# Two transformer blocks on one core: the recurrent mixer's gate chains are computed one head ahead, and the eight accumulator banks are divided anew

## The reference

```
h = rms_norm(x, attn_norm)
proj = h @ w_in                       # all projections of the layer
o_a = sparse attention, 4 heads of 128, keys chosen by a score (top 128)
o_b = hgrn2_mixer(q, f, i, g)         # 4 heads of 128, below
o_c = latent attention, 4 heads of 128 + 64 rotated
gates = sigmoid(proj[gate columns])   # 3 x 1024 columns
mixed = g_a * (o_a @ w_up_a) + g_b * (o_b @ w_up_b) + g_c * (o_c @ w_up_c)
x = x + mixed @ w_out
h = rms_norm(x, ffn_norm)
x = x + (silu(h @ w_ffn_gate) * (h @ w_ffn_up)) @ w_ffn_down    # width 2816
out = rms_norm(x, final_norm)

def hgrn2_mixer:                      # in chunks of 64 rows, a state per head
    log_f = logaddexp(log lb, log(1-lb) + log_sigmoid(f));  k = (1-lb) * sigmoid(-f)
    b = cumsum(log_f) within the chunk
    attn[t,s] = sum_k q[t] k[s] exp(b[t]-b[s]),  s <= t
    o = (q * exp(b)) @ state + attn @ v
    state = exp(b_last) * state + (k * exp(b_last - b))^T @ v
    out = rms_norm(o) * silu(g)
```

## Time and profile before

| | |
|---|---|
| Median of 3 runs | 2035.2 us (2034.4 to 2037.26) |
| The profiled execution: its time, and its span in the trace | 2032.24 us, 2030.4 us |
| PE busy | 1764.3 us (87% of the span) |
| PE clock granted, mean over the span | 0.933 of full speed |
| DVE, ACT, POOL busy | 847.8, 805.0, 590.5 us (42%, 40%, 29%) |
| Moved by transfers | 149.83 MB |

### The profile page before, as it was taken

One profiled execution on the slowest core, in us unless ns is written; L12 is line 12 of the kernel. 1 busy time (PEld: TensorE's weight loads), 2 busy tenths in 40 slices (PEclk: granted clock), 3 DMA queues, 4 the chain that ended last, 5 costly groups with the idle time before them and its releaser, 6 DMA issues.

```text
span 2030.4 us, 20883 instructions
## 1 busy us (share of the span) xinstructions
PE 1764.3 (87%) x7694; PEld 1325.3 (65%) x7694; DVE 847.8 (42%) x1477; ACT 805.0 (40%) x1512; POOL 590.5 (29%) x291
## 2 busy tenths in 40 slices
PE   4899998889989988889979968867769879999997
PEld 3666765667757656676636657656557658888886
DVE  4363345453433453544983536242326312212401
ACT  2234447322344563433324545453443324434411
POOL 4332211144122211422201222131236424444540
PEclk8898999999989988899989989888879989999999
DMA  5312221023132201231212222221245323333221
GB/s 172 88 42 63 63 59 57 22 64 93 32 82 54 83 32 43 88 82 33 60 36 58 73 73 63 60 66 48 66 132 185 103 62 100 98 94 101 86 94 42
DMA packets 204115, 149.83 MB, mean 74 GB/s; under 512 B 14956, under 2 KB 183536, under 8 KB 204016
## 3 DMA queue, kind: packets, MB, share of 16 engines
q1 hardware_dynamic: 199488, 133.57, 23.3%
q0 software_dynamic: 4528, 14.95, 2.4%
HBM read 138.00 MB, written 10.49 MB: 73 GB/s over the span
## 4 chain that ended last, share of the span: by engine, by line
PE 69%; DVE 13%; ACT 8%; issue 4%; DMA 3%; SPq 1%; POOL 0%; ACTq 0%; DVEq 0%
PE proj L1436 39%; PE proj L1432 12%; PE attn_out L1602 3%; PE score L1559 3%; PE score L1622 2%; PE turned_probs L1588 2%; PE proj L1622 1%; ACT weights_rounded L1900 1%; PE attn_out L1622 1%; DMA weights_raw<-in_w_in 1%; DVE small L2157 1%; DMA gates<-constants 1%; SPq L1316 1%; DVE rel_bias L2070 1%; PE score L1563 1%
## 5 line engine op out<-in xcount | busy, mean ns | idle before, releaser
L1378 POOL TENSOR_TENSOR weights_rounded<-weights_raw,weights_rounded 128x1024 fp32r<-128x1024 f32 (+1 forms) x237 | 562.8, 2392 | 1140.3 <-ACT weights_rounded L1900 1140.2
L1436 PE MATMUL proj<-hT_high,weights_rounded 128*128 128x512 f32 x2336 | 785.7, 410 | 47.4 <-DVE weights L2325 16.6
L1436 PEld LDWEIGHTS proj<-hT_high,weights_rounded 128*128 128x128 f32 x2336 | 456.9, 196 | 163.3 <-issue 20.4
L1436 PE MATMUL proj<-hT_low,weights_rounded 128*128 128x512 f32 x1168 | 468.9, 401 | 0.0
L1900 ACT ACTIVATE weights_rounded<-weights_raw 128x1024 fp32r<-128x1024 f32 (+1 forms) x237 | 233.9, 1009 | 161.1 <-DMA weights_raw<-in_w_ffn_down 57.8
L1436 PEld LDWEIGHTS proj<-hT_low,weights_rounded 128*128 128x128 f32 x1168 | 229.2, 196 | 50.4 <-issue 4.7
L1432 PE MATMUL proj<-weights_rounded,hT_high 128*128 128x512 f32 (+1 forms) x640 | 212.3, 409 | 43.8 <-DVE hT_low L1981 21.0
L1432 PEld LDWEIGHTS proj<-weights_rounded,hT_high 128*128 128x128 f32 x640 | 127.9, 203 | 77.3 <-issue 23.4
L1588 PE MATMUL turned_probs<-constants,probs 128*128 128x128 f32 x320 | 62.1, 296 | 43.4 <-ACT probs_T L1792 43.0
L1640 ACT ACTIVATE tg<-proj 128x512 f32<-128x512 f32 x42 | 25.1, 598 | 177.0 <-PE proj L1436 177.0
L1559 PE MATMUL score<-qk 64*128 64x256 f32 (+3 forms) x256 | 81.0, 495 | 11.0 <-DVE qk L1975 8.2
(11 more groups left out here) (371 smaller groups left out, 2463.6 us busy)
## 6 DMA issues: line engine op xcount, KB each, us to landing
weights_raw<-in_w_in SPq DMA_DIRECT2D x113, 512.0 KB, 4.1
weights_raw<-in_w_out SPq DMA_DIRECT2D x24, 512.0 KB, 3.8
weights_raw<-in_w_ffn_gate SPq DMA_DIRECT2D x22, 512.0 KB, 3.8
weights_raw<-in_w_ffn_up SPq DMA_DIRECT2D x22, 512.0 KB, 3.8
weights_raw<-in_w_ffn_down SPq DMA_DIRECT2D x22, 512.0 KB, 3.6
gates<-constants POOLq DMA_DIRECT2D x24, 256.0 KB, 2.4
weights_raw<-gates SPq DMA_DIRECT2D x24, 256.0 KB, 3.9
weights_raw<-in_w_in SPq DMA_DIRECT2D x20, 256.0 KB, 3.1
```

Of the source, the lines that this page charges most:

```text
L1378: nc.gpsimd.tensor_tensor(piece_view(WR, p, "raw"), piece_view(WF, p, "raw"), piece_view(WR, p, "high"), ALU.subtract).then_inc(w_low, 1)
L1436: mm = nc.tensor.matmul(ps[:, :], w_[:, c0:c0 + P], x_[:, k, :], start=first, stop=last)
```

## The change

Four things change together.

1. Until the last stage the projections have three banks and the scores two, instead of two and three.
2. The mixer stage is written by hand (`paced`): each job has a fixed number of ticks behind it. The hf and hq groups and the gate chain of head h + 1 stand among the levels of head h, with second copies of k, b and q (`by_head`). The put of a level stands ahead of the next level's work, and a `sigmoid` or projection group stands between most dependent steps, where state, out and meansq stood closer together. The mixer stage holds 22 gates, and two are left for the last stage.
3. In the last stage the groups go round all eight banks.
4. The first feed-forward chunk is done in two parts: the 384 columns of the first three row tiles before the last tile is turned (`early`), and 128 columns after it.

The steps of the first block and of the score stage keep their order.

```diff
-PROJ_BANKS = 2
-SCORE_BANKS = 3
+PROJ_BANKS = 3
+SCORE_BANKS = 2
+BANKS = 8
...
+    def paced(jobs, new_items):
+        add_items(new_items)
+        for fn, ticks in jobs:
+            fn()
+            for _ in range(ticks):
+                if state["n"] < len(items) + DRAIN:
+                    tick()
...
+    def hgrn_turn(h):
         put_back()
-        hold["put"] = g
+        group("hg_turn", head=h)
+        if h < 3:
+            steps.append(("hg_diff", (h + 1, 0)))
...
+    for h in range(4):
+        last = h == 3
...
+        level(-1, 1)
+        jobs.append((lambda h=h: next_f(h + 1), 0))
+        level(0, 1)
+        jobs.append((lambda h=h: next_q(h + 1), 0))
+        level(1, 0)
+        jobs.append((next_gate, 0))
+        jobs.append((lambda h=h: gate_step(h + 1, ("hg_gate_d", 0)), 0))
+        level(2, 1)
+        jobs.append((lambda h=h: gate_step(h + 1, ("hg_gate_a", 1)), 0))
+        level(3, 0)
+        jobs.append((next_gate, 1))
+        jobs.append((lambda h=h: gate_step(h + 1, ("hg_gate_d", 1)), 0))
+        level(4, 0)
+        jobs.append((lambda h=h: hgrn_gate(h), 1))
+        level(5, 1)
+        jobs.append((lambda: steps.append(("gate2", hold["g"])), 0))
+        jobs.append((next_gate, 0))
+        jobs.append((lambda h=h: hgrn_turn(h), 1))
+        jobs.append((lambda h=h: hgrn_state(h), 1))
+        jobs.append((next_gate, int(last)))
+        jobs.append((lambda h=h: hgrn_out(h), int(last)))
+        if not last:
+            jobs.append((next_gate, 0))
+        jobs.append((lambda h=h: hgrn_meansq(h), int(last)))
+        if not last:
+            jobs.append((next_gate, 0))
+        jobs.append((lambda h=h: hgrn_norm(h), 0))
+    paced(jobs, its)
     flush()
     state["after"] = ("tail", 0)
     steps.append(("tail", 0))
+    steps.append(("split_x", ("ya", 0, 4)))
+    while given[0] < N_GATES:
+        next_gate()
+    new_rings(RINGS_TAIL)
...
+    turned = [group("to_hT", tile=NT - 1, half=half, norm=2 * NT - 1, late=True) for half in range(2)]
+    begun = []
+    for what, name in (("ffgate", "ffg"), ("ffup", "ffu")):
+        sl = slab(name, at=0)
+        used(sl, turned[0])
+        begun.append(group(what, sl, K=KD, ring=0, late=True, cols=P * (NT - 1), **(dict(chunk=0, gate=begun[0]) if begun else {})))
+    steps.extend([("early", g) for g in begun] + [("group", g) for g in turned + begun])
...
+    for g in range(len(groups)):
+        b = g % PROJ_BANKS if tail_group is None or g < tail_group else (g - tail_group) % BANKS
...
-        hF, hA, hK, hQ = (qk[:, 4 + i, :] for i in range(4))
-        hB, hG, hQD, hKE, hATT = (X[:, i, :] for i in range(5))
+        hF, hA = qk[:, 4, :], qk[:, 5, :]
+        hB0, hG, hQD, hKE, hATT = (X[:, i, :] for i in range(5))
+        by_head = [(hB0, qk[:, 6, :], qk[:, 7, :]), (E[:, 0, 1, :], E[:, 1, 1, :], ikT)]
...
+                    elif bank_no[g] >= PROJ_BANKS:
+                        pe.wait_ge(exp_done, len(items))
+                        pe.wait_ge(soft1_done, soft1_at[-1])
+                        pe.wait_ge(turned_out, turned_at[-1])
...
+                    if lv == 0 and h:
+                        dve.wait_ge(group_full, out_group[h - 1] + 1)
```

More of the change, by code:

```diff
@@ L516, in plan @@
     if not only_block1:
-        second(steps, groups, slabs, items, units, state, slab, used, group, turn_rows, wide_tiles, weave, flush, new_rings, rounds)
+        second(steps, groups, slabs, items, units, state, slab, used, group, turn_rows, wide_tiles, weave, paced, flush, new_rings, rounds)
     place_splits(steps, groups, slabs, pieces)
@@ L551, in place_splits @@
         k = max(at.get(seq, -1), start[p["after"]], before)
-        while steps[k + 1][0] not in ("group", "half", "down"):
+        while steps[k + 1][0] not in ("group", "half", "early", "down"):
             k += 1
@@ L561, in place_splits, with second @@
     steps[:] = out
-def second(steps, groups, slabs, items, units, state, slab, used, group, turn_rows, wide_tiles, weave, flush, new_rings, rounds):
+def second(steps, groups, slabs, items, units, state, slab, used, group, turn_rows, wide_tiles, weave, paced, flush, new_rings, rounds):
     l = DEPTH
@@ L655, in hgrn_level @@
             steps.append(("hg_decay", h))
-        g = group("hg_attn", head=h, level=lv)
+        hold["put"] = group("hg_attn", head=h, level=lv)
+    def hgrn_turn(h):
         put_back()
-        hold["put"] = g
+        group("hg_turn", head=h)
+        if h < 3:
+            steps.append(("hg_diff", (h + 1, 0)))
     def hgrn_state(h):
-        group("hg_turn", head=h)
-        put_back()
-        if h < 3:
-            hgrn_q(h + 1)
-        gs = [group("hg_state", head=h, part=i) for i in range(2)]
@@ L666, in hgrn_state @@
-        if h < 3:
-            hgrn_f(h + 1)
-        steps.append(("hg_chain", (h, gs)))
-        hold["states"] = gs
-        if h < 3:
-            steps.append(("hg_gate_a", (h + 1, 0)))
-        hold["g"] = hgrn_gate(h)
-        if h < 3:
-            steps.append(("hg_gate_d", (h + 1, 0)))
+        hold["states"] = [group("hg_state", head=h, part=i) for i in range(2)]
+        steps.append(("hg_chain", (h, hold["states"])))
     def hgrn_out(h):
-        hold["hgout"] = group("hg_out", head=h, states=hold["states"])
@@ L678, in hgrn_out, with hgrn_meansq, hgrn_norm @@
-        if h < 3:
-            steps.append(("hg_gate_a", (h + 1, 1)))
+        group("hg_out", head=h, states=hold["states"])
+    def hgrn_meansq(h):
         group("hg_meansq", head=h)
+    def hgrn_norm(h):
         steps.append(("hg_norm", h))
         steps.append(("gate3", hold["g"]))
-        if h < 3:
-            steps.append(("hg_gate_d", (h + 1, 1)))
-            steps.append(("hg_diff", (h + 1, 0)))
     def hgrn_gate(h):
-        g = group("gate", slab("hgrn", c0=HG + 128 * h), K=KD, chunk=4 + h, layer=l, first=False, unit=None)
@@ L704, in gate_logs, with gate_step, next_f @@
-    def gate_logs(i):
-        if 0 <= i < N_GATES:
-            steps.append(("sig_ln", i))
-    def gate_out(i):
-        if 0 <= i < N_GATES:
-            steps.append(("sig_out", i))
+        put_back()
+        hold["g"] = group("gate", slab("hgrn", c0=HG + 128 * h), K=KD, chunk=4 + h, layer=l, first=False, unit=None)
+    def gate_step(h, *what):
+        if h < 4:
+            steps.extend((name, (h, part)) for name, part in what)
+    def next_f(h):
+        if h < 4:
+            put_back()
+            hgrn_f(h)
@@ L876, in annotate @@
             gr["vals"] = dict(values) if kind.startswith("hg_") else None
+        elif op == "early":
+            groups[arg]["early_hT"] = list(hT_groups)
         elif op == "split_x":
@@ L1250, in two_blocks @@
         ffup_group = [gr["g"] for gr in groups if gr["kind"] == "ffup"]
-        tail_group = next((gr["g"] for gr in groups if gr["kind"] == "up"), None)
         n_swaps = sum(gr["kind"] == "swap" for gr in groups)
@@ L1399, in _ @@
                     pe.wait_ge(prep, N_PREP)
-                elif op in ("group", "half"):
+                elif op in ("group", "half", "early"):
                     gr = groups[arg]
```

131 lines of the change are left out of this document (68 added, 63 removed).

## The result

The changed kernel takes 1960.47 us (median of 4 runs, 1960.21 to 1964.25), against 2036.23 us for the kernel before in runs beside it (4 runs, 2034.4 to 2037.5): ratio 0.9633, 95% interval 0.9616 to 0.965, faster. The forecast was 1948 us, 87 less than before; measured are 76 less. The profiled execution took 1960.21 us with a span of 1958.4 us, 72.0 us under the span of before.

The account below looks back on a forecast made before the run. PE's work plus its waits, densest in the mixer stage, bound the kernel. Mixer stage -82, way in +9, last stage -16 and first block +2 sum to -87 us, giving 1948 us; range 1912 to 1988.

Parts of the forecast that it names:

- Mixer stage: Groups and items ahead of dependent steps cover PE's waits; 9% idle, clock 0.95: 307 us, 82 less (64 to 123).
- the stores' pace: Rival, chance 0.22: in the mixer stage gates' copies wait for stores, costing most of 42 us: 1980 us.
- Way in: From the last `hg_out` to the first `up`: two leftover gates and waits for their weights, 9 us more.
- Last stage: Turned-tile waits gone, early part and split nearly even, some clock regained: 16 us less, 5 to 26.
- with eight banks PE no longer waits for the evacuation of a turned tile: In the last stage, PE's waits of 9.1 + 3.0 us for turned tiles' banks go.
- the 5 that I had counted for the clock: In the last stage, half of the 10 us lost at the lower clock level comes back: 5 us less.
- the late part: In the last stage, 48 matmuls of 128 columns at 0.112 us each take 5.4 us.
- First block: Only its banks change: 8 us for two score banks against 6 for the third projection bank, 2 more.
- The term for two score banks: In the first block, scores wait until the item two before lets go of its bank: 8 us more over two layers.
- The term for the third bank: In the first block, waits for spread rows (5.2) and copied values (3.0) go in part: 6 us less.
- everything is covered: Rival, chance 0.14: mixer stage with 3% idle and clock 0.98 takes 279 us, 28 less: 1920 us.
- the clock staying at 0.89: Rival, chance 0.06: PE's waits shorten but the clock falls as often as before; mixer stage 21 us more: 1974 us.

Follow-up runs that it names:

- experiment 3: The changed kernel with two projection banks and three score banks, in its new order: 1993.37 us, ratio 0.9821 to the kernel before.
- experiment 5: The changed kernel with three places instead of two for the tail gates' values: 1919.87 us, ratio 0.9462 to the kernel before.
- experiment 9: The kernel before, its order and banks kept, with three places for the tail gates' values: 2017.3 us, ratio 0.9935.
- Experiment 8: The changed kernel with its eight banks kept but the first feed-forward product in one part: 1956.74 us, ratio 0.9633 to the kernel before.
- experiment 1: The kernel before with three projection banks and two score banks, nothing else changed: 1988.29 us, ratio 0.9798.
- 4: The changed kernel with three banks in turn to the end and the first feed-forward product in one part: 1956.65 us, ratio 0.9641 to the kernel before.
- experiment 2: The kernel before with two score banks instead of three, the freed bank unused until `down`: 2044.53 us, ratio 1.0074.

## Why the prediction came out near

**Mixer stage: forecast 82 less, measured 60.2.** The mechanism was right: groups and items ahead of the dependent steps took away the waits for the put, the chain, the squares and the gate chain, and order and bank add (46 and 14 us, experiment 3). The step that failed is the one that gave the stores' pace a chance of its own instead of a term: the store's wait is there, and a chain that I held covered, turn, copy, state, hangs behind it. With it gone the stage takes 303.3 us (experiment 5), 101 less than before. That is within the ends of 64 and 123 that I had named. So of 101 us that order, bank and a third place give together, 41 hung on the stores. My price for that rival, 42 us, was right in sum and by luck, as I had 34 of idle time and 8 of the clock, and measured are 21.6 and 19.2. I had also taken its base too high, since idle came to 6% and the clock to 0.98 where I chose 9% and 0.95. Two choices between far ends, both toward the worse, stood in for the wait that I left out of the sum. The old order gained only 13 us by a third place (experiment 9), perhaps as it asked for gates less evenly and PE stood for other chains meanwhile; that last reason is argued, not shown.

**Way in: forecast 9 more, measured 11.3.** I had 8.5 us of PE waiting for the leftover gates' weights and found 12.69. I had listed the copy, the branch's rounding, the logs and exponential, the rounding and POOL. Missing was DVE: its 2.29 us for the branch's low part stand ahead of the gate's minimum, and the logs wait for that:

```profile
1415.70 1.91 ACT L1968 ACTIVATE branches_high<-y 128x2048 fp32r<-128x2048 f32 x1 [1.09 <-DVE y L2109]
...
1417.65 2.29 DVE L2422 TENSOR_TENSOR branches_low<-y,branches_high 128x2048 fp32r<-128x2048 f32 x1 [2.06 <-ACT branches_high L1968]
1419.86 0.69 DVE L2091 SCALAR_TENSOR_TENSOR constants<-constants,gate_logs 128x512 f32<-128x512 f32 x1
1420.63 0.63 ACT L1690 ACTIVATE gate_logs<-constants 128x512 f32<-128x512 f32 x1 [3.02 <-DVE constants L2091]
...
1423.01 1.99 ACT L1952 ACTIVATE weights_rounded<-weights_raw 128x1024 fp32r<-128x1024 f32 x2
...
1426.67 0.76 PE L1488 MATMUL proj<-hT_high,weights_rounded 128*128 128x512 f32 x1 [12.69 <-POOL weights_rounded L1422]
```

ACT's waits of 3.02 us for that chain and of 1.09 for the norm ahead of the branch's rounding are the missing 4.2. The wait ahead of `up` is 2.97 us, forecast near 3. Another of 3.39 us for POOL, 9 us behind the first `up`, I had not foreseen; it lies in the last stage.

**Last stage: forecast 16 less, measured 6.9.** The step that failed is "with eight banks PE no longer waits for the evacuation of a turned tile", taken as worth 9.1 + 3.0 us. These waits are gone, but waits for data stood behind them, and PE waits for those now. Experiment 8 has the eight banks and the product whole, and its list has these:

```profile
PE proj L1478 <- DVE mix_low L2416: 3.6, 3, 3.1
PE proj L1536 <- DVE logits L2308: 3.4, 1, 3.4
```

Its idle time from the first `up` to the first `down` is 18.8 us against 25.7 before, 7 less instead of 12. Its busy time is 5.1 less (364.5 to 359.3), which are the 5 that I had counted for the clock. Nor does it take eight banks: in experiment 1, with three in turn, the stretch from the first `up` to the first feed-forward product is 134.1 us against 146.9 before, and 1.0 us is left of these waits. Eight instead of three bring nothing that can be seen (experiment 8 against 4). The second term that was off is the late part. I had the waits right in kind and nearly in size, 4.81 and 1.67 us for my 4 and 2, but sized the work behind them at the full clock; and they took 10.2 us instead of 5.4. In the profiles the split costs 9.0 us of work against my 2.7 and saves 3.8 of idle time against my 2.0, so a cost of 0.7 became one of 5.2. Of the 6.3 us more work the late part is 4.8. The rule of the Trainium skill that I had set beside this term (TensorE: Matmul & The Clock Gate, Back-to-back issue gap: about 81 ns for 128 columns) was further off than the row: the first products came every 0.11 us at full clock, and 48 in 10.2 us are 213 ns each, most of them at the lower level.

**First block: forecast 2 more, measured 10.8 less.** The term for two score banks was right: 8 forecast, 9.3 measured (experiment 2), with the wait at 320.76 of 5.54 us where I had read 5.6, and again in the second layer. The term for the third bank was not: 6 forecast, 22.1 measured. I had looked only for waits that named a copy out of a bank, ACT's of the spread rows and values. The twelve waits for turned rows' low part looked like waits for data in the list of before:

```profile
PE proj L1432 <- DVE hT_low L1981: 21.0, 12, 7.6
```

Eight of them went with the third bank, so they were for a full bank. The rest of the 22.1 us is the spread rows and values, smaller waits, and 7.6 us of busy time. The same step failed in the score stage, where I had 0 and the third bank gave 5.5 (161.3 to 155.8): DVE does hold PE at the end, but full banks held it before.

**The other rivals.** That everything is covered did not come; experiment 5 shows what kept it away. Against the clock staying at 0.89 stands 0.92 in this kernel and 0.98 with the stores' wait gone. That the clock simply follows the waits is not so, though: in the new order the bank edits took 13.2 us of idle time away and left it at 0.92 (experiment 3 against the changed kernel). The bank cycling that the Trainium skill names (same page, A second HAM failure mode: psum-queue depth-cycling) shows no effect here either: with eight banks in turn the feed-forward from 1600 to 1700 has 1.00, as with two before.

```profile
1600.00:1700.00 100.00, 100.00 (x443) 82.78 (x442) 28.02 (x35) 43.77 (x63) 46.40 (x18) 1.00 0.33 95
```

What stays open: why the bank edits and the new order add so exactly in the mixer stage, and why the clock rose to 0.98 with one kind of wait and stayed at 0.92 with another. The parts of the new order (the gate chain ahead, the put, the gates between dependent steps) were only run together, so what each gave is not shown. The order of a gate's exponential ahead of the next gate's logs, which would start each store 1.9 us earlier with two places, wasn't tried.

## What to carry to other kernels

When a change packs independent work into an engine's waits, ask what that work itself needs: here each gate moved into a gap held a place until its store had landed, and ACT, which serves everything in order, passed that wait on to the chain that the change had shortened. A wait for data that recurs where a bank is about to be filled again can be a wait for the bank; try one more buffer of each kind alone before reordering. Splitting a product to fill a wait makes short products, and these can run at the lower clock: here they took nearly twice what I had sized, in all five executions that had them.

## What the runs showed of the hardware

- A wait can cost about its length again through the clock, or next to nothing: one more place for the gates took 21.6 us of idle time and 19.2 us of busy time out of the same stage and the same instructions, with the granted clock going from 0.92 to 0.98. The bank edits took 13.2 us of idle time and 1.1 of busy time out of that stage, with the clock at 0.92 before and after.
- 48 products of 128 columns behind waits of 4.81 and 1.67 us took 10.2 us, with PE busy in the whole of it and a granted clock of 0.50 from 1585 to 1598. The first few came every 0.11 us, the others every 0.21.
- The stores of 256 KB are not cheap to wait for: 68.6 us in 19 waits, 3.6 us each. At the place shown POOL issued the store at once, at 1210.42, and ACT went on at 1214.92, 4.5 us later; the queue of POOL, which I had put into the rival's price, had no part in that one.
